# One core, Trainium2: attention's outputs made transposed, four column tiles for the state space's outputs, and the last team's sum split in two pairs

## The chip, the cores and the metric

One core of one Trainium2 chip. The metric is the device time of one execution in microseconds (us), smaller is better. Engines: TensorE (PE; its weight loads are shown as PEld), VectorE (DVE), ScalarE (ACT), GpSimd (POOL), and the queue that SyncE issues transfers on (SPq). All data are float32, for which every matrix product of the program is two instructions on TensorE, and a transpose one.

## The reference

One layer over 320 tokens: 256 of a prompt and 64 of a sample. Every token goes through three branches, gated and summed, then through a mixture of experts.

```python
h = rmsnorm(x, g_attn); proj = h @ w_in          # u, q_lat, kv_lat, k_pe, q_mem, gate logits
# A: s5_branch(u): diagonal complex state space, 32 groups of 16 channels, 64 states each
#    h_t = ab * h_{t-1} + bu_t;  y = Re(c h) + d u;  out = GLU(gelu(y) @ w_glu)
# B: o = softmax(q k^T / sqrt(96), chunk mask) v, 8 heads of 64;  @ w_o_mla
# C: o = softmax(q_mem mem_k^T / sqrt(128)) mem_v, 4 heads of 128;  @ w_o_mem
x = x + (gA * br_a + gB * br_b + gC * br_c) @ w_out
# experts: 4 groups of 8; a token's best group, its two best experts there
x = x + sum_e gate_e * ((silu(h2 @ w_e1[e]) * (h2 @ w_e3[e])) @ w_e2[e])     # 32 experts, 1024 -> 256 -> 1024
```

## The kernel before

Tokens stand in three tiles (`TILES`): two of 128 for the prompt and a short one of 64 for the sample (`t` = 0, 1, 2). Weights come through three slots `W0` to `W2`; later seven slots `E13` hold experts' up-weights (2 MB an expert, in two transfers) and six slots `E2` down-weights (1 MB).

**The middle.** `middle()` (from L188) writes out one list of steps, `MIDDLE`, and each engine runs the same list in this order and does its part of each step. `put` appends a step and adds its `WORK` to `spent`; when `spent` reaches `due`, `start_turn` puts a turn of the state space in. So a step more or less in the list moves the turns against the other steps. Results in PSUM rotate over five banks (`RING`), and a bank is written again when its former content was copied out (`emptied`, by the engine that `emptier` names).

**Attention.** The heads of a tile are cut into units, 5 for `mem` (branch C) and 10 for `mla` (branch B). A unit m has the steps S (scores), PT (transposes of the probabilities P) and O (output), in the order S(n), PT(n-1), O(n-2), with fills between them (`gateC`, `gateB`, `gateA`: 16 instructions of 320 columns each). After S VectorE takes the maximum (`scores_max`), ScalarE the exponentials P with their sums; PT waits for these. O is made with tokens on the rows: weights PT, moving the values (L966). VectorE divides by the sums when it copies O out (L1749, L1753). When a tile's O is whole, a step OT transposes it (four instructions, L926) and ScalarE copies it to `oTmem` or `oTmla`.

**The state space.** There are 16 turns. `turn_in(q)`: TensorE makes the inputs of turn q (`s5_turn`, L894 and L895, 32 rows deep each, in different row tiles and banks), VectorE rotates them by four products and two sums (L1681 to L1688); `turn_scan` (L1698) twice; `turn_back` (L1706 to L1715) writes a state in `hS[q % 4]`. In each odd turn from 3 on, `s5_y` (L883) multiplies two finished states by `wC`, each onto 32 of 128 rows of bank `YB`, so four turns fill it; `y_skip` on VectorE takes it up. `last_y` does the last two states.

**The end of the middle.** `LAST_WOUT` is the last product with `w_out`. The loads of the experts 4 to 6 wait for it on SyncE (`done(LAST_WOUT[NT - 1])`), since their slots lie where the weights were. Routing follows.

**The experts.** Pairs p = 0 to 15, two pairs a team of 128 rows. For each pair TensorE does `up(p)` (64 instructions of 256 columns onto 32 rows each, four column tiles), `hid_transpose`, `down(p)` (16 of 512 columns, L1217), between these the former team's sums into X (`add_team`, `sum_products`, L1227; VectorE adds them to X, L2080) and the next team's rows. `load_up(e)` waits until `up` has used the slot, `load_down(e)` likewise. The last expert's weights come in halves with semaphores of their own. After `down(15)` the last team's sums are made in five steps (`SUMS`): weights `WG` 128 deep, which is both pairs' rows of `yb` at once; VectorE adds all of them to X and SyncE stores X in five transfers (L621).

```python
for n in range(len(units) + 2):                       # attention_order
    if n < len(units): yield "S", n
    if 1 <= n <= len(units): yield "PT", n - 1
    if n >= 2:
        yield "O", n - 2
        if n - 1 == len(units) or units[n - 1][1] != units[n - 2][1]:
            yield "OT", units[n - 2][1]
```

## Time and profile before

| what | value |
|---|---|
| median of 3 runs | 646.52 us (645.71 to 647.54) |
| profiled execution | 645.93 us, its span 644.1 us |
| TensorE busy | 611.7 us, 95% of the span |
| VectorE, ScalarE, GpSimd busy | 329.3, 170.9, 149.7 us |
| chain that ended last | TensorE 83%, transfers' queue 9%, VectorE 4% |
| moved by DMA | 150.55 MB, 147.12 MB of it read |
| granted TensorE clock | 0.999 of full speed |

The span is that of the profiled execution; busy time is what the engine spent in instructions, so a busy TensorE may still be one that fills few of its rows. The chain follows the last instruction back to what released each step. A row of a timeline gives the start in us, the time in us, engine, line, operation, written and read tiles, rows and columns, how many instructions were merged, and in brackets the idle time before it with what ended it.

### The profile page before, as it was taken

The page shows a single profiled execution, that of the slowest core. Times are in us where ns is not written, and L with a number is a line of the kernel's source. Part 1 is how long each engine was busy: PE and PEld are TensorE (multiplying, and loading weights), DVE is VectorE, ACT ScalarE, POOL GpSimd, SP SyncE. Part 2 cuts the span into 40 slices and gives each one's busy share as a digit, 9 for nine tenths or more (in the row PEclk, how much of TensorE's full clock was granted, in tenths as well). Part 3 has the DMA queues.
Part 4 walks back from the last instruction along what each step waited for, and adds up shares of the span by engine and source line. Part 5 has one row for each costly group of instructions (what it writes and reads, how often), then busy time and mean ns, then how long its engine had stood idle before and what let it go on. Part 6 is the DMA issues. An engine that isn't in the chain of part 4 may idle for free.

```text
span 644.1 us, 9883 instructions
## 1 busy us (share of the span) xinstructions
PE 611.7 (95%) x3674; PEld 378.5 (59%) x3674; DVE 329.3 (51%) x878; ACT 170.9 (27%) x540; POOL 149.7 (23%) x341
## 2 busy tenths in 40 slices
PE   9999999999999999999999999998999999986785
PEld 6788867776556667666677767853443343332341
DVE  2434846868874588783133322675435335334233
ACT  5534234321678433221100101121221121120100
POOL 1695726733584433410000000000000000000000
PEclk9999999999999999999999999999999999999999
DMA  9783553222301523323389991098999999999993
GB/s 301 176 284 115 193 159 99 66 67 93 101 2 33 168 95 99 99 66 98 107 236 404 399 386 64 10 383 345 417 417 413 418 416 417 417 418 417 416 409 126
DMA packets 61681, 150.55 MB, mean 234 GB/s; under 512 B 12352, under 2 KB 40448, under 8 KB 53696
## 3 DMA queue, kind: packets, MB, share of 16 engines
q1 hardware_dynamic: 61632, 149.89, 62.7%
q8 instruction: 31, 0.51, 0.3%
q14 instruction: 18, 0.15, 0.1%
HBM read 147.12 MB, written 2.76 MB: 233 GB/s over the span
## 4 chain that ended last, share of the span: by engine, by line
PE 83%; SPq 9%; DVE 4%; DMA 2%; ACT 1%; issue 1%
PE PS L819 30%; PE PS L829 20%; SPq L704 6%; PE PS L1188 5%; PE PS L1096 5%; PE PS L1227 3%; SPq L708 3%; PE PS L1217 3%; DMA E<-in_w_e 2%; PE PS L943 2%; PE PS L966 2%; PE PS L894 2%; PE PS L883 1%; PE PS L800 1%; PE PS L1008 1%; PE PS L951 1%
## 5 line engine op out<-in xcount | busy, mean ns | idle before, releaser
L819 PE MATMUL PS<-hT,W 128*128 128x320 f32 x448 | 125.9, 436 | 0.0
L819 PEld LDWEIGHTS PS<-hT,W 128*128 128x128 f32 x448 | 83.6, 190 | 37.5 <-issue 5.2
L1188 PE MATMUL PS<-E,xT 128*32 128x256 f32 x1024 | 58.6, 379 | 9.5 <-issue 8.4
L1188 PEld LDWEIGHTS PS<-E,xT 128*32 128x32 f32 x1024 | 35.4, 110 | 36.9 <-issue 20.4
L2152 POOL TENSOR_SCALAR means<-sums 128x4 f32<-128x4 f32 (+3 forms) x35 | 7.9, 225 | 189.2 <-ACT junk L1325 188.2
L1096 PE MATMUL PS<-h,S 128*128 128x512 f32 (+1 forms) x96 | 48.2, 625 | 0.7 <-DVE S L1939 0.7
L1227 PE MATMUL PS<-yb,WG 128*128 128x512 f32 (+1 forms) x96 | 40.9, 622 | 4.0 <-DVE X L2080 3.1
L829 PE MATMUL PS<-W,hT 128*128 128x256 f32 (+5 forms) x256 | 41.7, 353 | 0.0
L2080 DVE TENSOR_TENSOR X<-X,PS 128x512 f32<-128x512 f32 (+1 forms) x48 | 32.9, 686 | 8.3 <-PE PS L1227 6.7
L829 PEld LDWEIGHTS PS<-W,hT 128*128 128x128 f32 (+1 forms) x256 | 31.5, 163 | 8.4 <-issue 1.3
L829 PE MATMUL PS<-W,mergedT 128*128 128x384 f32 (+3 forms) x192 | 35.7, 381 | 0.0
L819 PE MATMUL PS<-uT,W 128*128 128x320 f32 x128 | 34.6, 432 | 0.0
L1217 PE MATMUL PS<-E,hidT 128*32 128x512 f32 x256 | 31.0, 598 | 2.6 <-issue 2.0
L2062 DVE COPY yb<-PS 64x512 f32<-64x512 f32 x16 | 10.9, 684 | 41.2 <-PE PS L1217 41.2
L1096 PEld LDWEIGHTS PS<-h,S 128*128 128x128 f32 (+1 forms) x96 | 15.5, 187 | 27.9 <-issue 26.7
L2153 POOL TENSOR_TENSOR rstd<-means,halves 128x4 f32<-128x4 f32 (+3 forms) x35 | 31.0, 885 | 2.9
L819 PEld LDWEIGHTS PS<-uT,W 128*128 128x128 f32 x128 | 24.3, 190 | 10.1
L829 PEld LDWEIGHTS PS<-W,mergedT 128*128 128x128 f32 (+1 forms) x192 | 24.2, 163 | 9.8 <-issue 0.3
L829 PE MATMUL PS<-W,memT 128*128 128x256 f32 x128 | 28.3, 381 | 0.0
L1227 PEld LDWEIGHTS PS<-yb,WG 128*128 128x128 f32 (+1 forms) x96 | 11.4, 170 | 28.0 <-DVE X L2080 15.4
L1421 ACT ACTIVATE P<-PS,soft 128x256 f32<-128x256 f32 (+2 forms) x30 | 13.3, 450 | 49.6 <-DVE soft L1744 21.8
L829 PEld LDWEIGHTS PS<-W,memT 128*128 128x128 f32 x128 | 24.1, 190 | 4.0 <-issue 0.9
(313 smaller groups left out, 959.0 us busy)
## 6 DMA issues: line engine op xcount, KB each, us to landing
E<-in_w_e SPq DMA_DIRECT2D x93, 1024.0 KB, 21.8
W<-in_w_in SPq DMA_DIRECT2D x7, 1536.0 KB, 7.2
W<-in_w_in SPq DMA_DIRECT2D x7, 1024.0 KB, 6.6
W<-in_w_mem_kv SPq DMA_DIRECT2D x4, 1024.0 KB, 6.1
W<-in_w_glu SPq DMA_DIRECT2D x4, 768.0 KB, 8.0
W<-in_w_out SPq DMA_DIRECT2D x2, 1536.0 KB, 15.4
E<-in_w_e SPq DMA_DIRECT2D x6, 512.0 KB, 18.8
X<-in_x_prompt SPq DMA_DIRECT2D x4, 512.0 KB, 4.4
```

Source lines behind the costliest of these rows:

```text
L704: sp.dma_start(E13[e % UPS][:, n, k0:k1, :], e13_src[n][:, e, k0:k1, :]) .then_inc(up_loaded[e % UPS] if k0 == 0 else s["last_up_loaded"], 16)
L708: sp.dma_start(E2[e % DOWNS][:, j0:j1, :], e2_src[:, e, j0:j1, :]) .then_inc(down_loaded[e % DOWNS] if j0 == 0 else s["last_down_loaded"], 16)
L819: ins = mm(out[:, 0:TOK], w[:, k, cols:cols + 128], rhs[:, k, :], start=(k == 0), stop=(k == kt - 1))
L829: ins = mm(out[r:r + n, 0:part.stop - part.start], lhs[:, k, f:f + n], w[:, k, c0 + part.start:c0 + part.stop], start=(k == 0), stop=(k == ...
L894: mm(PS[:, BU, 0:TOK], wB[r:r + 32, 0, t, :], uT[r:r + 32, t, :], start=True, stop=True)
L1096: return mm(PS[:, banks + c, :], S[0:n, t, :], h2[0:n, t, 512 * c:512 * c + 512], start=(t == 0), stop=(t == NT - 1))
L1188: ins = mm(PS[r:r + B, 2 + par, 0:FF], xT[:, k, place_ + B * n:place_ + B * n + B], E13[slot][:, :, k, 128 * j:128 * j + 128], start=(k == ...
L1217: ins = mm(PS[r:r + B, 5, :], hidT[:, par, 64 * n + B * j:64 * n + B * j + B], E2[slot][:, j, 512 * c:512 * c + 512], start=(j == 0), stop ...
L1227: ins = mm(PS[r:r + rows_, sum_bank(n), :], WG[:, f:f + rows_], yb[:, c, :], start=True, stop=True)
L1421: ins = fn(P[0:n, m % 2, nk * h:nk * h + nk], src[0:n, nk * h:nk * h + nk], ACT.Exp, bias=soft[0:n, w, 0, h:h + 1], scale=scale, accum_out ...
L2080: yield V_.tensor_tensor(x, x, PS[r:r + rows_, sum_bank(n), :], ALU.add)
L2153: g_.tensor_tensor(rstd[0:rows_, n, 0:heads], means[0:rows_, n, 0:heads], halves[0:rows_, 0:heads], ALU.pow)\
```

## The change

- **Attention.** The steps OT go. O is now made transposed: the values are the weights and PT moves, so the result has features on the rows: 128 of them a head in `mem`, in `mla` two heads side by side in column tiles of 64. ScalarE copies it straight to `oTmem` or `oTmla`. The division by the sums moves before the transposes: VectorE multiplies P in place (`shares(m)`), in its part of step S of unit m+1, for the last unit in its own PT. PT waits for `shares_ready`.
- **State space.** `s5_y(t)` takes four states at once onto four column tiles, in turns 5, 9, 13 and in `last_y`; `hS` has five buffers (`STATES`).
- **Last team.** Before `up(15)`, TensorE puts columns 0 to 511 of X (times the identity) and the share of pair 14 of four of the six results in PSUM (`rows_so_far`, `add_last_but_one`); the other two come around `hid_transpose(15)`. `down(15)` works in halves of 256 columns into banks 5 and 4, which VectorE and ScalarE copy 128 rows high. `add_last` adds pair 15, 64 deep, alternating row tiles; ScalarE copies columns 0 to 511 to X, VectorE adds columns 512 to 1023, and SyncE stores six parts.
- **Loads.** Up-weights of expert 30 are loaded after the down-weights of 28 and 29; those of expert 31 as 6/8 and 2/8.

```diff
+STATES = 5
...
-            if n - 1 == len(units) or units[n - 1][1] != units[n - 2][1]:
-                yield "OT", units[n - 2][1]
...
-            if step == "OT":
-                whole.append(m)
-                continue
...
-                for k0, k1 in ((0, KD),) if e < NE - 1 else ((0, KD // 2), (KD // 2, KD)):
+                for k0, k1 in ((0, KD),) if e < NE - 1 else ((0, LAST_K), (LAST_K, KD)):
...
-                if 2 * p + UPS < NE:
+                ups, downs = (range(2 * p + n, min(2 * p + 2 + n, NE)) for n in (UPS, DOWNS))
+                if ups:
                     sp.wait_ge(s["ab_full"], p + 1)
-                    for e in range(2 * p, min(2 * p + 2, NE - UPS)):
-                        load_up(e + UPS)
-                if 2 * p + DOWNS < NE:
+                for e in ups:
+                    if e != NE - 2:
+                        load_up(e)
+                if downs:
                     sp.wait_ge(s["y_mm"], p + 1)
-                    for e in range(2 * p, min(2 * p + 2, NE - DOWNS)):
-                        load_down(e + DOWNS)
+                for e in downs:
+                    load_down(e)
+                if NE - 2 in ups:
+                    load_up(NE - 2)
...
-            for n, (t, cs) in enumerate(SUMS):
+            for i, t in enumerate(LAST_TILES):
                 f, rows_ = TILES[t]
-                sp.wait_ge(s["sum_added"], added_by(len(SUMS) * (TEAMS - 1) + n))
                 dst = o["y_p"][f:f + rows_, :] if t < 2 else o["y_s"]
-                c0, c1 = 512 * cs[0], 512 * cs[-1] + 512
-                store(dst[:, c0:c1], X[0:rows_, t, c0:c1])
+                for c, by in enumerate(("last_act", "last_dve")):
+                    sp.wait_ge(s[by], i + 1)
+                    store(dst[:, 512 * c:512 * c + 512], X[0:rows_, t, 512 * c:512 * c + 512])
             st.after(stored[-1])
...
-            def s5_y(q):
-
-                t = q // 4
-                pe.wait_ge(s["h_state"], q + 2)
-                if q % 4 == 0 and t > 0:
+            def s5_y(t):
+
+                pe.wait_ge(s["h_state"], 4 * t + 4)
+                if t > 0:
                     pe.wait_ge(s["y_skipped"], t)
                 for c in range(2):
-                    for n in (q, q + 1):
-                        r = 32 * (n % 4)
-                        ins = mm(PS[r:r + 32, YB, 0:TOK], wC[:, c, t, r:r + 32], hS[:, n % 4, c, :], start=(c == 0), stop=(c == 1))
+                    for n in range(4):
+                        r = 32 * n
+                        ins = mm(PS[r:r + 32, YB, 0:TOK], wC[:, c, t, r:r + 32], hS[:, (4 * t + n) % STATES, c, :], start=(c == 0), stop=(c == 1))
...
-                if q % 2 == 1 and q > 1:
-                    s5_y(q - 3)
+                if q % 4 == 1 and q > 1:
+                    s5_y(q // 4 - 1)
...
-                        emptied((kind, "S", m))
+                        pe.wait_ge(s["shares_ready"], unit0 + m + 1)
...
-                        dv = MD if mem_ else VH
-                        for x in range(nh):
+                        across_ = 1 if mem_ else 2
+                        for i in range(heads // across_):
                             for b, rows_ in enumerate(kb):
-                                for c in range(parts):
-                                    h = h0 + nh * c + x
+                                for r in range(across_):
+                                    c, x = divmod(across_ * i + r, nh)
+                                    h = h0 + across_ * i + r
                                     at = 128 * (x * len(kb) + b) + n * c
                                     if mem_:
-                                        rhs = mv[0:rows_, t // 2, b, MD * h:MD * h + MD]
+                                        values = mv[0:rows_, t // 2, b, MD * h:MD * h + MD]
                                     else:
-                                        rhs = V[0:rows_, (0 if t < 2 else 2) + b, VH * h:VH * h + VH]
-                                    ins = mm(out[n * c:n * c + n, dv * x:dv * x + dv], PT[0:rows_, m % 2, at:at + n], rhs,
+                                        values = V[0:rows_, (0 if t < 2 else 2) + b, VH * h:VH * h + VH]
+                                    w = 128 // across_
+                                    ins = mm(out[w * r:w * r + w, n * i:n * i + n], values, PT[0:rows_, m % 2, at:at + n],
...
+            def last_down(slots, par):
 
                 for j in range(2):
-                    if j == 1 and second is not None:
-                        pe.wait_ge(*second)
+                    if j == 1:
+                        pe.wait_ge(s["last_down_loaded"], 16)
+                    for half, bank_ in enumerate((5, 4)):
+                        for c in range(2):
+                            for n, slot in enumerate(slots):
+                                r, at = 64 * c + B * n, 512 * c + 256 * half
+                                ins = mm(PS[r:r + B, bank_, 0:256], hidT[:, par, 64 * n + B * j:64 * n + B * j + B],
+                                         E2[slot][:, j, at:at + 256], start=(j == 0), stop=(j == 1))
...
+            def last_place(t, c):
+                bank_, r = LAST_BANKS[t, c]
+                return PS[r:r + TILES[t][1], bank_, :]
+
+            def rows_so_far():
+
+                pe.wait_ge(s["sum_added"], ADDS * (TEAMS - 1))
+                pe.wait_ge(s["weights_ready"], TEAMS)
+                pe.wait_ge(s["weights_moved"], 1)
+                for t in LAST_TILES:
+                    n = TILES[t][1]
+                    mm(last_place(t, 0), ident[0:n, 0:n], X[0:n, t, 0:512], start=True, stop=False)
+
+            def add_last_but_one(t, c):
+                f, n = TILES[t]
+                mm(last_place(t, c), WG[0:64, f:f + n], yb[0:64, c, :], start=(c == 1), stop=False)
+
+            def add_last():
+                pe.wait_ge(s["last_y"], 2)
+                for t in LAST_TILES:
+                    f, n = TILES[t]
+                    for c, weights in enumerate((last_weights[:, f:f + n], WG[64:128, f:f + n])):
+                        mm(last_place(t, c), weights, last_rows[64 * c:64 * c + 64, :], start=False, stop=True).then_inc(s["last_full"], 1)
...
+                    rows_so_far()
+                    pe.wait_ge(s["y_dve"], PAIRS - 1)
+                    pe.wait_ge(s["y_act"], PAIRS - 1)
+                    for t in LAST_TILES[0:2]:
+                        for c in range(2):
+                            add_last_but_one(t, c)
                 up(p)
+                if p == PAIRS - 1:
+                    add_last_but_one(LAST_TILES[2], 0)
...
+                    add_last_but_one(LAST_TILES[2], 1)
                 down(p)
-            add_team(TEAMS - 1, range(len(SUMS)))
+            add_last()
...
+                def shares(m):
+                    _, nh = across(units[m])
+                    nk = sum(key_blocks(units[m]))
+                    w = soft[:, (unit0 + m) % 4]
+                    dve.wait_ge(*emptied_at(UNIT_NO[kind, "S", m]))
+                    link(V_.reciprocal(w[:, 2, 0:nh], w[:, 1, 0:nh]))
+                    p = P[:, m % 2, 0:nh * nk].rearrange("p (h k) -> p h k", h=nh)
+                    V_.tensor_tensor(p, p, w[:, 2, 0:nh, None].broadcast_to([128, nh, nk]), ALU.mult).then_inc(s["shares_ready"], 1)
+
+                if step == "PT" and m == len(units) - 1:
+                    shares(m)
                 if step == "S":
+                    if m > 0:
+                        shares(m - 1)
...
-                    link(V_.reciprocal(w[:, 2, 0:nh], w[:, 1, 0:nh]))
-                    n = TILES[t][1]
-                    for c in range(parts):
-                        h, r = h0 + nh * c, slice(n * c, n * c + n)
-                        st.mark(V_.tensor_tensor(O[0:n, t, dv * h:dv * (h + nh)].rearrange("p (h d) -> p h d", h=nh), src[r],
-                                                 w[r, 2, 0:nh, None].broadcast_to([n, nh, dv]), ALU.mult),
-                                s["emptied_dve"] if c == parts - 1 else None)
...
+                    V_.tensor_copy(last_rows[:, 0:256], PS[:, 5, 0:256]).then_inc(s["last_y"], 1)
...
-            add_team(TEAMS - 1, range(len(SUMS)))
+            for i, t in enumerate(LAST_TILES):
+                bank_, r = LAST_BANKS[t, 1]
+                n = TILES[t][1]
+                dve.wait_ge(s["last_full"], 2 * i + 2)
+                V_.tensor_tensor(X[0:n, t, 512:D], X[0:n, t, 512:D], PS[r:r + n, bank_, :], ALU.add).then_inc(s["last_dve"], 1)
```

**Order of VectorE, the last unit of `mem`.** Before, around turn 6 (L1681 to L1688 are `turn_in`, L1743 and L1744 the maximum of the last S, L1749 and L1753 the division of an O, L1698 `turn_scan`):

```order
L1743 TENSOR_REDUCE soft<-PS 128x2 [waits psum_full]
L1744 TENSOR_SCALAR soft<-soft 128x2 [waits dve_step]
L1749 RECIPROCAL soft<-soft 128x2 [waits psum_full]
L1753 TENSOR_TENSOR O<-PS,soft 128x256 [waits dve_step]
L1681 TENSOR_TENSOR rotA<-PS,tab_133 128x320 [waits bu_full,turn_tables]
L1682 TENSOR_TENSOR rotB<-PS,tab_133 128x320
L1683 TENSOR_TENSOR rotA<-PS,tab_133 128x320
L1684 TENSOR_TENSOR rotB<-PS,tab_133 128x320
L1686 TENSOR_TENSOR rotA<-rotA,rotB 128x320 [waits dve_step]
L1688 TENSOR_TENSOR rotA<-rotA,rotB 128x320 [waits dve_step,bu_free]
L1698 SCALAR_TENSOR_TENSOR rotB<-s5tmp,rotA 128x256 [waits dve_step]
L1698 SCALAR_TENSOR_TENSOR rotB<-s5tmp,s5par,rotA 128x64
```

The scans follow the turn directly. Now the same place (L1728 to L1735 and L1801, L1802; L1781 and L1783 are `shares`, first of unit 3, then of unit 4):

```order
L1781 RECIPROCAL soft<-soft 128x2 [waits emptied_act]
L1783 TENSOR_TENSOR P<-P,soft 128x512 [waits dve_step]
L1801 TENSOR_REDUCE soft<-PS 128x2 [waits psum_full]
L1802 TENSOR_SCALAR soft<-soft 128x2 [waits dve_step]
L1728 TENSOR_TENSOR rotA<-PS,tab_132 128x320 [waits bu_full,turn_tables]
L1729 TENSOR_TENSOR rotB<-PS,tab_132 128x320
L1730 TENSOR_TENSOR rotA<-PS,tab_132 128x320
L1731 TENSOR_TENSOR rotB<-PS,tab_132 128x320
L1733 TENSOR_TENSOR rotA<-rotA,rotB 128x320 [waits dve_step]
L1735 TENSOR_TENSOR rotA<-rotA,rotB 128x320 [waits dve_step,bu_free]
L1781 RECIPROCAL soft<-soft 128x2 [waits emptied_act]
L1783 TENSOR_TENSOR P<-P,soft 128x512 [waits dve_step]
```

The divisions of O are gone from behind the maximum and the scans. Shares 3 stands before the maximum, and shares 4, for which the last PT waits, stands directly behind the whole of `turn_in 6`.

**Order of TensorE at the same place.** L819 and L814 are gates, L894/L895 and L888/L889 the turn, L926 an OT, L951 and L939 the transposes of P, L966 and L956 the O. Before, from OT of tile 0:

```order
L926 MATMUL PS<-cst,O 128x128 [waits emptied_dve,emptied_act]
L926 MATMUL PS<-cst,O 128x128 x3
L951 MATMUL PS<-cst,P 128x128 [waits emptied_act]
L951 MATMUL PS<-cst,P 128x128 x3
L966 MATMUL PS<-mv,PT 128x128 [waits emptied_act,emptied_dve]
L966 MATMUL PS<-mv,PT 128x128 x3
L894 MATMUL PS<-uT,wB 128x320 [waits bu_free]
L895 MATMUL PS<-crossed_146,wB 128x320
L819 MATMUL PS<-hT,W_145 128x320 [waits emptied_act,chunk_loaded2]
L819 MATMUL PS<-hT,W_145 128x320 x7
L951 MATMUL PS<-cst,P 128x128 [waits emptied_act]
L951 MATMUL PS<-cst,P 128x128 x3
```

A gate stands between the turn and PT 4. Now, from the transposes of unit 3:

```order
L939 MATMUL PS<-cst,P 128x128 [waits shares_ready,emptied_act]
L939 MATMUL PS<-cst,P 128x128 x3
L956 MATMUL PS<-PT,mv 128x128 [waits emptied_act]
L956 MATMUL PS<-PT,mv 128x128 x3
L814 MATMUL PS<-hT,W_144 128x320 [waits emptied_act,chunk_loaded2]
L814 MATMUL PS<-hT,W_144 128x320 x7
L888 MATMUL PS<-uT,wB 128x320 [waits bu_free]
L889 MATMUL PS<-crossed_145,wB 128x320
L939 MATMUL PS<-cst,P 128x128 [waits shares_ready,emptied_act]
L939 MATMUL PS<-cst,P 128x128 x3
L956 MATMUL PS<-PT,mv 128x128 [waits emptied_act]
L956 MATMUL PS<-PT,mv 128x128 x3
```

The gate (gateC 3) has moved ahead of the turn, and PT 4 follows the turn at once.

**Order of TensorE at the end.** Now, from the last two y products of pair 14 to the first product of `up(15)` (L1255 `rows_so_far`, L1259 `add_last_but_one`, L1178 `up`):

```order
L1218 MATMUL PS<-E_4_157,hidT 32x512
L1218 MATMUL PS<-E_5_158,hidT 32x512
L1272 TENSOR_LOAD ovi [waits ov_ready]
L1272 ISA x2
L1255 MATMUL PS<-X,cst 64x512 [waits weights_moved,weights_ready,sum_added]
L1255 MATMUL PS<-X,cst 128x512 x2
L1259 MATMUL PS<-yb,WG 64x512 [waits y_act,y_dve]
L1259 MATMUL PS<-yb,WG 64x512
L1259 MATMUL PS<-yb,WG 128x512 x2
L1178 MATMUL PS<-E_2_153,xT 32x256 [waits xt_ready,hid_ready,up_loaded3,up_loaded2]
```

Before, `up(15)` followed the y products of pair 14 directly; seven products of 512 columns stand between them now.

## Rows read from the trace of the kernel before

**Rows 1.** table of stretches (us: engines' busy us, clock, DMA share, GB/s)

```profile
35.00:421.00 386.00, 384.88 (x1927) 268.99 (x1925) 218.93 (x567) 115.66 (x421) 133.72 (x294) 1.00 0.43 144
390.00:417.00 27.00, 27.00 (x196) 20.73 (x194) 11.67 (x45) 4.47 (x8) 1.51 (x4) 1.00 0.00 1
...
440.00:600.00 160.00, 147.20 (x1261) 63.35 (x1254) 67.95 (x176) 27.59 (x56) 0.00 (x0) 1.00 1.02 417
```

**Rows 2.** chain that ended last, from 616 us (start us, us, what)

```profile
616.86 15.23 DMA E<-in_w_e
...
634.11 4.72 PE PS L1227 x12
...
638.86 0.69 DVE X L2080
```

**Rows 3.** timeline of TensorE, turn 13

```profile
262.29 0.53 PE L894 MATMUL PS<-uT,wB 32*128 32x320 f32 x1
...
263.03 1.27 PE L883 MATMUL PS<-hS,wC 128*32 128x320 f32 x8
264.23 0.66 PE L951 MATMUL PS<-cst,P 128*128 128x128 f32 x4
```

**Rows 4.** timeline of TensorE, second half of `up(15)`

```profile
627.19 1.93 PE L1188 MATMUL PS<-E,xT 128*32 128x256 f32 x32 [0.68 <-DMA E<-in_w_e]
```

**Rows 5.** timeline of TensorE, OT 0, PT 3, O 2 and S 5 of `mla`

```profile
255.26 0.60 PE L926 MATMUL PS<-cst,O 128*128 128x128 f32 x4
255.69 0.60 PE L951 MATMUL PS<-cst,P 128*128 128x128 f32 x4
256.13 1.00 PE L966 MATMUL PS<-V,PT 128*128 128x64 f32 x8
256.97 1.08 PE L943 MATMUL PS<-kT,qT 96*128 96x256 f32 x4
```

**Rows 6.** timeline of TensorE, O of the last unit of `mem`

```profile
147.71 1.09 PE L966 MATMUL PS<-mv,PT 128*64 128x128 f32 x16
148.73 0.53 PE L894 MATMUL PS<-uT,wB 32*128 32x320 f32 x1
```

**Rows 7.** timeline of VectorE, `mla`, before the maximum of unit 4

```profile
252.60 0.15 DVE L1749 RECIPROCAL soft<-soft 128x4 f32<-128x4 f32 x1
252.79 0.42 DVE L1753 TENSOR_TENSOR O<-PS,soft 128x256 f32<-128x256 f32 x1
...
253.97 0.68 DVE L1740 SCALAR_TENSOR_TENSOR PS<-PS,early 128x512 f32<-128x512 f32 x1
```

**Rows 8.** groups of VectorE by form (busy us, mean ns, idle before)

```profile
L1792 DVE TENSOR_TENSOR KQ<-KQ,rstd 128x384 f32<-128x384 f32 x4 | 2.2, 556 | 2.9 <-POOL rstd L2153 2.8
```

**Rows 9.** timeline of TensorE: turn 4, PT 0 and PT 1 of `mem`

```profile
109.90 0.53 PE L894 MATMUL PS<-uT,wB 32*128 32x320 f32 x1
...
113.81 0.66 PE L951 MATMUL PS<-cst,P 128*128 128x128 f32 x4
...
119.48 0.60 PE L951 MATMUL PS<-cst,P 128*128 128x128 f32 x4
```

**Rows 10.** timeline of VectorE: `turn_in 4`, maximum of S 1, of S 2

```profile
110.83 0.49 DVE L1681 TENSOR_TENSOR rotA<-PS,tab 128x320 f32<-128x320 f32 x1 [3.80 <-PE PS L895]
...
113.42 0.68 DVE L1743 TENSOR_REDUCE soft<-PS 128x2 f32<-128x512 f32 x1
...
120.06 0.68 DVE L1743 TENSOR_REDUCE soft<-PS 128x2 f32<-128x512 f32 x1
```

**Rows 11.** timeline of TensorE, pair 14's transposes and y products, pair 15's

```profile
621.05 0.62 PE L1160 MATMUL PS<-cst,Sg 128*128 128x128 f32 x3
622.03 1.92 PE L1217 MATMUL PS<-E,hidT 128*32 128x512 f32 x16 [0.36 <-issue]
...
631.02 2.18 PE L1217 MATMUL PS<-E,hidT 128*32 128x512 f32 x16 [0.54 <-DMA E<-in_w_e]
```

**Rows 12.** stores from X on SyncE's queue (ns; first and last start)

```profile
L621 SPq DMA_DIRECT2D out_y_p<-X x4: 417/493/576, 637.4 to 639.6; - x4
```

More of the change, by code:

```diff
@@ L263, in middle @@
             fill()
-    whole = attention("mem", MEM_UNITS, 1)
+    attention("mem", MEM_UNITS, 1)
     for t in range(NT):
@@ L271, in middle @@
         put("qlT", t)
-    for t in whole:
-        put("mem", "OT", t)
     for j in range(len(KEYS)):
@@ L288, in middle @@
     held, pace, due = False, LATE_PACE, spent
-    whole = attention("mla", MLA_UNITS, 1)
+    attention("mla", MLA_UNITS, 1)
     fill(1)
-    for t in whole:
-        put("mla", "OT", t)
     while turn < GP:
@@ L343, in emptier @@
     if unit[0] in ("mem", "mla"):
[L344 removed]
+        return "act"
     return "dve" if unit[0].startswith("out") else "act"
@@ L719, in _ @@
             sp.dma_start(brow[:, NG:], a["b_re"][0].rearrange("g e -> (g e)").partition_broadcast(128)).then_inc(s["router_loaded"], 16)
-            done(("mla", "OT", NT - 1))
+            done(("mla", "O", len(MLA_UNITS) - 1))
             load_up(0)
@@ L921, in attention @@
                     out = begin((kind, step, m))
-                    if step == "OT":
-                        n = TILES[m][1]
-                        emptied((kind, "O", max(k for k, x in enumerate(units) if x[1] == m)))
-                        for j in range(4):
-                            ins = nc.tensor.transpose(out[:, n * j:n * j + n], O[0:n, m, 128 * j:128 * j + 128], ident[0:n, 0:n])
-                        end(ins)
-                        return
-                    _, t, h0, nh = units[m]
+                    unit0 = 0 if mem_ else len(MEM_UNITS)
+                    _, t, h0, heads = units[m]
                     f, n = TILES[t]
@@ L1019, in branch @@
                     if d == 0:
-                        emptied(("mem" if kind == "outC" else "mla", "OT", NT - 1))
+                        emptied(("mem", "O", len(MEM_UNITS) - 1) if kind == "outC" else ("mla", "O", len(MLA_UNITS) - 1))
                     feature_major((kind, d), use(f"{kind}{g}"), col, oTmem if kind == "outC" else oTmla, 4)
@@ L1042, in _ @@
                 elif kind == "last_y":
-                    s5_y(GP - 2)
+                    s5_y(GP // 4 - 1)
             pe.wait_ge(s["z_ready"], 4)
@@ L1406, in attention @@
                 unit0, oT = (0, oTmem) if kind == "mem" else (len(MEM_UNITS), oTmla)
-                if step == "OT":
-                    f, n = TILES[m]
-                    empty(oT[:, :, f:f + n], full((kind, "OT", m))[:, 0:4 * n].rearrange("p (j n) -> p j n", j=4))
+                t, n = units[m][1], 128
+                if step == "O":
+                    f, n = TILES[t]
+                    j0, nj = (x * (MD if kind == "mem" else VH) // 128 for x in units[m][2:])
+                    empty(oT[:, j0:j0 + nj, f:f + n], full((kind, "O", m))[:, 0:nj * n].rearrange("p (j n) -> p j n", j=nj))
                     return
-                t, n = units[m][1], 128
                 _, nh = across(units[m])
@@ L1726, in attention @@
             def attention(kind, units, step, m):
[L1727 to L1728 removed]
                 unit0 = 0 if kind == "mem" else len(MEM_UNITS)
[L1730 to L1735 removed]
+                def shares(m):
[8 more added lines that the diff above has]
+                    shares(m)
+                if step == "S":
+                    if m > 0:
+                        shares(m - 1)
+                    t, n = units[m][1], 128
+                    _, nh = across(units[m])
+                    nk = sum(key_blocks(units[m]))
+                    w = soft[:, (unit0 + m) % 4]
                     src = full((kind, "S", m))[:, 0:nh * nk]
```

75 lines of the change are left out of this document (40 added, 35 removed).

## The prediction

> **What bounds the kernel now.** I read the table of stretches first, then the chain that ended last, then the timelines at the places that the diff touches. From 35 to 421 us TensorE is busy 384.9 of 386.0 us [rows 1]: a microsecond less of its work there, or a microsecond of waiting more, is a microsecond of time. From 390 to 417 us the DMA engines move nothing, because the loads of experts 4 to 6 wait for `done(LAST_WOUT...)`; from 440 us on they are busy without a gap at 417 GB/s [rows 1]. So the middle sets when the last stream of expert weights begins, the stream sets when it ends, and a shift of the middle goes through to the end whole. The chain ends with the last landing at 616.86 + 15.23 = 632.09 us, the last team's products from 634.11 (4.71 us) and a VectorE addition from 638.86 to 639.55 [rows 2]. What follows is stores. The profiled execution took 645.93 us (span 644.1); the median is 646.52, 0.6 above. The sum is made against 645.93 and then moved by 0.6.
>
> **The change, part by part: TensorE work that goes.**
> State-space output: a call of `s5_y` now is 8 instructions, two column tiles wide, and lasts 264.23 - 263.03 = 1.20 us [rows 3]. There are eight calls (64 instructions). The new call has 16 instructions, four column tiles wide. That four run side by side is seen in the experts: 32 instructions of 256 columns onto 32 rows take 1.93 us [rows 4], 0.06 each, so 16 of 320 columns take 16 x 0.06 x 320/256 = 1.2 us. Four calls fewer: **-4.8** (ends -4.4 and -5.0).
> Transposes of O ("OT"): four of them take 255.69 - 255.26 = 0.43 us [rows 5], six groups: **-2.6**.
> O of the prompt tiles in `mla`: 8 instructions now take 256.97 - 256.13 = 0.84 us, 0.105 each although only 64 columns stream [rows 5]; with operands swapped they have 64-row outputs and 128 columns, two side by side, as the 16 at 147.71 have: (148.73 - 147.71)/16 = 0.064 [rows 6]. 8 x 0.064 = 0.51, six units: **-2.0**. The last `mem` unit goes the other way: its 16 now fill all 128 output rows with 64 columns, at 0.105 instead of 0.064: **+0.7**.
> Together -8.7 us of TensorE work.
>
> **What it adds: a VectorE step before the transposes of P.** Until now a PT (the transposes of the probabilities P) waited for ScalarE's exponentials alone; now it waits for `shares_ready`. `shares(m)` is a reciprocal, 0.2 us until the next can start (252.60 to 252.79) [rows 7], and a multiplication of 128x512: 128x384 takes 0.56 and 128x256 0.42 [rows 7, 8], so 0.70 here. Ready 0.9 us after VectorE gets to it; VectorE itself is held 0.8. VectorE runs in order, and the turns' work stands ahead of it:
> - PT 0 of `mem`. Turn 4 on TensorE starts at 109.90 and on VectorE at 110.83; VectorE is through at 113.42, where share 0 now begins; ready 114.35. TensorE is there at 113.81 [rows 9, 10]: wait 0.55.
> - PT 1. Share 1 stands behind the whole of turn 4, which ended at 120.06 [rows 10]. With share 0 ahead: 120.06 + 0.8 + 0.9 = 121.8; TensorE is there at 119.48 + 0.55 = 120.0 [rows 9]: wait 1.8.
> - PT 4 of `mem`, the last unit. By the order, `turn_in 6` now stands directly before it, on TensorE and on VectorE (it stood before gateC 3). VectorE begins a turn 0.93 us after TensorE does and needs 113.42 - 110.83 = 2.6 for it [rows 9, 10], then the share 0.9: ready 4.4 us after the turn's start. TensorE needs 0.74 for the turn [rows 3]: wait **3.7**. Nothing covers it.
> - PT 3 of `mla`. VectorE begins the mask of unit 4 at 253.97 without idling before it [rows 7]. Shares 1 and 2 are added before it (+1.6), the normalisations of O 0 and O 1 go (2 x (0.2 + 0.35) = -1.1), and share 3 comes: ready at 255.4. TensorE, which gets to PT 3 at 255.69 now [rows 5], arrives earlier by one `s5_y` call (1.2), one OT (0.43) and two O (0.66): 253.4. Wait 2.0. The second gate behind it needs a PSUM bank whose exponentials are late by as much: 0.5 more.
> Elsewhere in both attentions a PT has a gate (4.4 us) between itself and the S that releases the share, and VectorE has caught up.
> Together **+8.5**. Ends: 3.7 alone, if VectorE keeps up elsewhere (its work beside GpSimd's between 115 and 119 us is stretched, and may stretch less), and 11, if the multiplications are stretched as those were. I take the sum by rows. ScalarE takes over the eviction of O: 15 copies instead of 6, against waits of microseconds there; nothing. The fifth state buffer lets `turn_back` run as before; nothing. The middle nets **-0.2**.
>
> **The end.** Loads: up-weights of expert 30 now come behind down-weights 28 and 29, and expert 31's come as 6/8 and 2/8. The bytes are the same, the last landing stays; the y products of pair 14 no longer wait. In its place TensorE gets work. After the transposes at 621.05 (0.62) [rows 11] come the y products of pair 14, 1.9 us [rows 11], to 623.6. Then, ahead of `up(15)`: three products of the identity with X, and four of pair 14's rows, of which the two of the short tile run side by side. That is six slots of 2 x 512 columns; the 12 instructions from 634.11 are ten such half slots in 4.71 us with 0.2 of latency [rows 2], so 0.43 to 0.45 a half slot, 0.86 a slot: 5.2 us. `up(15)` starts at 628.8, not in two halves at the landings; its 64 instructions take 3.7, to 632.4. Now it ends at 627.19 + 1.93 = 629.12 [rows 4]. From there to the y products is 631.02 - 629.12 = 1.9 [rows 11]: 634.3; two more products of pair 14 lie beside ScalarE's and VectorE's work in it. These are 32 of 256 columns, 1.9 [rows 4]: 636.2. The copies are halved, 0.42 instead of 0.69: 636.6, and 0.15 to TensorE: 636.8. Last products: six slots of 64 rows deep, two side by side in row tiles. The turn shows such pairs: 2 pairs of 320 columns take 263.03 - 262.29 = 0.74 [rows 3], 0.37 a pair, 0.10 above the streaming alone (0.27). So 6 x (0.43 + 0.10) + 0.2 = 3.4 (ends 2.8 with no loss, 5.2 with no overlap): 640.2. VectorE adds until 640.9, against 639.55 [rows 2]. Stores: the last was issued at 639.6 and one takes 0.5 [rows 12]; ScalarE's and VectorE's halves of the last tile are now ready together and the second is issued about 641.4. So the end is **+1.8** (ends +1.2 and +3.6), not the gain of about 1.1 that the shorter last products would give if `up(15)` still started at its landing.
> The Trainium skill, TensorEngine Tiling (Array Packing), section Restrictions and Gotchas, says that different row tiles have to write to different PSUM banks. The short tile's two last products are in different row tiles and share bank 6. By that rule they would not overlap, and the sum would be 0.4 us higher; the turn's pairs write to two banks, so no row here tests it.
>
> **Sum.** -8.7 + 8.5 + 1.8 = +1.6: 645.93 + 1.6 = 647.5 for the profiled execution, **648.1** beside the median.
>
> **The rivals.**
> 1. Slower: the waits on the shares grow. Between 115 and 120 us VectorE's scans and products took longer than elsewhere; if the 512-wide multiplications of five `mem` units are stretched by half, the waits grow by 1 to 1.5, and with the last products overlapping poorly (+1.5) it is 650.6. It decides from 0.4 us above the sum. For it: VectorE is what every PT waits for now. Against: most shares have a gate's cover.
> 2. Only the wait behind turn 6 is left, since VectorE has caught up at the other three: -8.7 + 3.7 + 1.8 = -3.2, 643.3. Against it: VectorE had no idle time before 120.06 and 253.97.
> 3. The end gains after all, because `up(15)` starts near its landing: -0.2 - 1.1, 645.2. It needs the seven inserted products to take 2 us instead of 5.2.
> 4. The change does all that it says and no wait shows: -8.7 - 1.1, 636.7. Turn 6 speaks against it by order, not by speed.
> 5. It doesn't do what it says: the four column tiles run two wide. Each of four calls lasts 2.4: no gain of 4.8, 652.9. The experts' 32-row products speak against it.
>
> **How the numbers follow.** About 0.3% (1.9 us) is what a measurement of this kernel can tell from no change. The sum as worked has 0.60, with 646.7 to 650 as its own spread; its middle lies 0.3 us under the bound to slower, so 0.38 of it is within and 0.22 above. Rival 1 has 0.15, rival 2 0.10, rivals 3 and 4 0.06 each, rival 5 0.03. Faster: 0.16; within: 0.44; slower: 0.40. The range from 643.2 (rival 2) to 650.6 (rival 1) leaves out rivals 4 and 5 and half of rival 1's worse side.
>
> **What would show it.** `s5_y` as four groups of 16 at 1.2 us; no transposes of O; the waits of TensorE on VectorE's P in 90 to 292 us together about 8, the longest 3.7 right behind turn 6; the stream of expert 4 beginning at 417, within half a microsecond; `up(15)` about 3 us after its weights; the last products in 3.4 us. Wrong would be: that wait under 2 us, or `up(15)` beginning before 627, or last products over 4.5.

## The result and the profile after

The changed kernel takes 650.62 us (median of 5 runs, 649.45 to 650.69), 4.1 us more than the 646.52 before; the ratio is 1.0058, 95% interval 1.0046 to 1.0070. It is **slower by 0.6%**. Its profiled execution took 650.69 us (span 648.8), 4.8 more than the one before. TensorE is busy longer than the 611.7 us before, although it has some 8 us less to do in the middle and some 6 us more in the last team, and the mean granted clock fell from 0.999 to 0.988. From the page (busy time by engine, and the chain that ended last, where before TensorE had 83% and the transfers' queue 9%):

```profile
PE 615.8 (95%) x3684; PEld 377.4 (58%) x3684; DVE 328.1 (51%) x870; ACT 174.3 (27%) x553; POOL 151.4 (23%) x341
...
PE 86%; DVE 9%; issue 2%; ACT 2%; DMA 1%; POOL 0%; SPq 0%; DVEq 0%; ACTq 0%
```

The stretches of the changed kernel (columns as in [rows 1], so TensorE's clock is the third from the right) show where:

```profile
140.00:145.00 5.00, 3.05 (x13) 1.63 (x11) 1.83 (x5) 0.44 (x1) 0.00 (x0) 1.00 0.20 81
145.00:150.00 5.00, 3.40 (x14) 3.24 (x15) 4.86 (x13) 0.98 (x2) 0.00 (x0) 0.50 0.00 0
150.00:155.00 5.00, 5.00 (x18) 3.35 (x17) 1.41 (x4) 0.00 (x0) 3.82 (x11) 0.82 0.00 0
```

TensorE idles 3.5 us, and from 145.0 us, still in that wait, to 151.7 its granted clock is 0.50, which is 1.2 GHz. No such stretch lies in the middle of the kernel before. This is about half of what the mean clock lost; the rest is two stretches among the experts, from 442 to 446 and from 585 to 589 us. Behind the second TensorE still idles 1.76 us before `up(13)` and again before `up(14)`, so these two do not reach the end. TensorE's waits by line (us in total, times, longest), and its timeline at this place:

```profile
PE PS L939 <- DVE P L1783: 6.9, 4, 3.5
PE PS L814 <- ACT P L1458: 0.2, 1, 0.2
```

```profile
142.62 0.43 PE L888 MATMUL PS<-uT,wB 32*128 32x320 f32 x1
...
146.60 1.09 PE L939 MATMUL PS<-cst,P 128*128 128x128 f32 x4 [3.54 <-DVE P L1783]
147.48 1.92 PE L956 MATMUL PS<-PT,mv 128*128 128x128 f32 x8
149.19 5.79 PE L814 MATMUL PS<-hT,W 128*128 128x320 f32 x16
154.81 1.89 PE L956 MATMUL PS<-PT,mv 128*128 128x64 f32 x16
156.63 0.53 PE L888 MATMUL PS<-uT,wB 32*128 32x320 f32 x1
```

The wait in brackets is the one behind turn 6. VectorE at the same place goes through the turn and then makes the last unit's shares, without idling between them:

```profile
143.17 0.49 DVE L1728 TENSOR_TENSOR rotA<-PS,tab 128x320 f32<-128x320 f32 x1 [9.19 <-PE PS L889]
...
145.57 0.15 DVE L1781 RECIPROCAL soft<-soft 128x2 f32<-128x2 f32 x1
145.76 0.69 DVE L1783 TENSOR_TENSOR P<-P,soft 128x512 f32<-128x512 f32 x1
```

The transposes behind it take 1.09 us, against 0.60 to 0.66 for such a group before [rows 9]; with the O, the gate and the last O it is 10.0 us from 146.60 to 156.63. At half clock from 146.6 to 151.7, TensorE did in 5.1 us what takes half of that at full clock: 2.5 us lost. The stream of experts 4 to 6 on SyncE's queue starts at 419.56 here:

```profile
419.56 21.01 SPq L695 DMA_DIRECT2D E<-in_w_e  x10
```

Before, it started at 417.09:

```profile
417.09 20.99 SPq L704 DMA_DIRECT2D E<-in_w_e  x10
```

So **2.5 of the 4.8 us are lost by the end of the middle**, and 2.3 in the last team: VectorE's last sum ends at 644.37 instead of 639.55 [rows 2], 4.8 later. The chain of waits at the end, from the y products of pair 14, is TensorE's work and VectorE's copy and sum, with no landing in it:

```profile
624.51 1.85 PE PS L1218 x16
626.36 2.91 PE PS L1255 x6
629.28 2.92 PE PS L1259 x8
632.19 3.59 PE PS L1178 x64
635.78 1.05 PE PS L1259 x2
636.84 0.32 PE PS L1187
637.15 1.05 PE PS L1259 x2
638.21 1.91 PE PS L1208 x32
640.12 0.02 issue
640.14 0.43 DVE xg L2111
640.57 0.04 issue
640.62 3.04 PE PS L1266 x12
643.66 0.02 issue
643.68 0.69 DVE X L2156
```

The last landing, which was the first link before [rows 2], is no part of it. `up(15)` starts 5.83 us behind the end of the y products of pair 14 (632.19 - 626.36).

### The profile page after: what moved, and what is told of

Read it like the earlier page. It is cut to its first block, busy times and chain, and to the rows that moved or that the text cites. A ratio compares the mean times of both kernels' runs of the same rounds, so it can differ in the third digit from the quotient of the medians.

```text
span 648.8 us, 9903 instructions
## 1 busy us (share of the span) xinstructions
PE 615.8 (95%) x3684; PEld 377.4 (58%) x3684; DVE 328.1 (51%) x870; ACT 174.3 (27%) x553; POOL 151.4 (23%) x341
## 4 chain that ended last, share of the span: by engine, by line
PE 86%; DVE 9%; issue 2%; ACT 2%; DMA 1%; POOL 0%; SPq 0%; DVEq 0%; ACTq 0%
PE PS L814 27%; PE PS L824 20%; PE PS L1178 8%; PE PS L1086 7%; PE PS L1218 5%; PE PS L1228 4%; PE PS L888 2%; PE PS L956 2%; DVE X L2131 1%; PE PS L1139 1%; PE PS L931 1%; PE PS L998 1%; DVE rotB L1745 1%; PE PS L939 1%; PE PS L1259 1%
## 5 line engine op out<-in xcount | busy, mean ns | idle before, releaser
L814 PE MATMUL PS<-hT,W 128*128 128x320 f32 x448 | 127.2, 439 | 0.2 <-ACT P L1458 0.2
L814 PEld LDWEIGHTS PS<-hT,W 128*128 128x128 f32 x448 | 84.4, 192 | 38.1 <-issue 6.2
L1178 PE MATMUL PS<-E,xT 128*32 128x256 f32 x1024 | 60.0, 387 | 6.9 <-issue 6.6
L1178 PEld LDWEIGHTS PS<-E,xT 128*32 128x32 f32 x1024 | 35.8, 112 | 35.8 <-issue 19.0
L1228 PE MATMUL PS<-yb,WG 128*128 128x512 f32 (+1 forms) x84 | 36.2, 625 | 3.1 <-DVE X L2131 3.1
L814 PE MATMUL PS<-uT,W 128*128 128x320 f32 x128 | 34.6, 432 | 0.0
L2131 DVE TENSOR_TENSOR X<-X,PS 128x512 f32<-128x512 f32 (+1 forms) x42 | 28.8, 686 | 6.8 <-PE PS L1228 5.3
L814 PEld LDWEIGHTS PS<-uT,W 128*128 128x128 f32 x128 | 24.3, 190 | 10.1
L2282 POOL TENSOR_TENSOR turnt<-tab 128x64 f32<-128x64 f32 (+2 forms) x48 | 25.4, 530 | 3.8
```

Source lines behind the costliest of these rows:

```text
L814: ins = mm(out[:, 0:TOK], w[:, k, cols:cols + 128], rhs[:, k, :], start=(k == 0), stop=(k == kt - 1))
L1178: ins = mm(PS[r:r + B, 2 + par, 0:FF], xT[:, k, place_ + B * n:place_ + B * n + B], E13[slot][:, :, k, 128 * j:128 * j + 128], start=(k == ...
L1228: ins = mm(PS[r:r + rows_, sum_bank(n), :], WG[:, f:f + rows_], yb[:, c, :], start=True, stop=True)
L2131: yield V_.tensor_tensor(x, x, PS[r:r + rows_, sum_bank(n), :], ALU.add)
L2282: st.mark(tt(t1, T[:, :, 0:n], cn, ALU.mult))
```

## The experiments

The medians stand against 647.0 to 647.1 us for the kernel before, measured beside them (645.1 to 647.8). Its runs lie in two groups, up to 646.7 and from 647.1 on, so a difference of medians is good to about half a microsecond only. Four runs took the change apart, four took the waits and the tail apart, four followed up.

The profiles give a sharper figure for the middle: the time from the start of turn 0 on TensorE to the start of the stream of experts 4 to 6. It leaves out what differs before turn 0, and it is 361.21 us in all four profiles that have the middle of before.

| kernel | turn 0 | stream | between | against before |
|---|---|---|---|---|
| before | 55.88 | 417.09 | 361.21 | |
| `tail_only`, `tail_no_identity`, `order_of_loads` | 56.67, 56.87, 57.06 | 417.88, 418.08, 418.27 | 361.21 | 0 |
| changed | 56.35 | 419.56 | 363.21 | +2.0 |
| `mid_only` | 56.49 | 419.94 | 363.45 | +2.2 |
| `s5_only` | 56.55 | 413.02 | 356.47 | -4.7 |
| `att_only` | 56.02 | 421.97 | 365.95 | +4.7 |
| `turn_later` | 56.39 | 413.55 | 357.16 | -4.1 |
| `shares_sooner` | 56.48 | 413.34 | 356.86 | -4.4 |
| `mid_shares_sooner` | 56.25 | 411.54 | 355.29 | -5.9 |
| `shorter_wait` | 56.86 | 415.92 | 359.06 | -2.2 |
| `pace_12_5` | 56.45 | 409.18 | 352.73 | -8.5 |
| `pace_11_5` | 56.56 | 413.06 | 356.50 | -4.7 |

**The two halves of the program.** `mid_only` is the changed kernel with the last team of before; `tail_only` the reverse.

```diff
-            add_last()
+            add_team(TEAMS - 1, range(len(SUMS)))
```

(for `mid_only`, with its loads, copies and stores.)

> The change's attention and state-space parts, with the last team, its loads and its sums as in the kernel before. Theory: the middle loses by itself. In the changed kernel's trace the stream of experts 4 to 6 begins at 419.56 us against 417.09, 2.5 later, of which 0.5 had gone before 35 us, where both run the same instructions. So 2.0 to 2.5 above before: 648.5 to 649.1, the wait behind turn 6 about 3.5 us, and the granted clock at half speed for some 6 us right behind it. Rival: only the tail costs, the late stream being made up in its waits for landings: 646.5, with a stream that begins late all the same.

Measured: 648.99 (647.65 to 649.80), ratio 1.0033 [1.0021, 1.0044], **+2.0**. The stream starts at 419.94, the wait is 3.55, the clock is at half from 145.6 to 152.0 us. The rival falls: the late stream is not made up, the last landing is at 635.27 against 632.09.

> The kernel before with only the change's last team: its loads, the seven products ahead of up(15), the halved copies, the split sum. Theory: the inserted products delay up(15) by their own length whether or not the middle is late. The changed kernel's last VectorE addition ends at 644.37 against 639.55, 4.8 later, less the 2.5 of the stream: +2.3, so 648.8 (648.4 to 649.2), with up(15) starting about 5.8 us behind the end of pair 14's y products. Rival: the tail is a gain (shorter last products, 3.0 instead of 4.7) and only looks late because the middle was: 645.2 to 646.5.

Measured: 650.10 (649.51 to 650.38), ratio 1.0051 [1.0037, 1.0065], **+3.1**, more than the theory's 2.3. `up(15)` starts 5.83 us behind the y products as expected, and VectorE's last sum ends at 642.32; with the stream 0.8 late (417.88), that is 2.0 above before. The rest is behind it: in this profile one of the four stores of the prompt took 1.77 us to issue, in the changed kernel none over 0.59.

```profile
L624 SPq DMA_DIRECT2D out_y_p<-X x4: 446/516/1772, 641.6 to 643.2; - x4
```

(ns, smallest, median, largest.) Whether every run of `tail_only` has that isn't known (all six lie within 0.9 us); it would explain why the two halves sum to 5.0 and the whole is 4.1.

**The two parts of the middle.** `s5_only` is the kernel before with the new `s5_y(t)` and this in place of the eight calls (the fourth is in `last_y`):

```diff
+STATES = 4
...
-                if q % 2 == 1 and q > 1:
-                    s5_y(q - 3)
+                if q % 4 == 0 and q > 0:
+                    s5_y(q // 4 - 1)
```

> The kernel before with s5_y on four column tiles, four calls instead of eight; with O still in memory a fifth state buffer does not fit, so there are four buffers and the call stands in turns 4, 8 and 12 (three states old at least by a whole turn) and in last_y. Theory: TensorE is full in the middle and each call that goes is 1.2 us: -4.8, 641.7 (641.2 to 642.3), the stream beginning at 412.3. Rival: the freed time turns into waits on VectorE, which runs the turns, or on the ring: 643.5 or more.

Measured: 642.11 (640.85 to 643.04), ratio 0.9929 [0.9913, 0.9945], **-4.9**, and the middle is 4.7 shorter in the profile. The theory's -4.8 holds.

`att_only` has the attention hunks and `s5_y(q)` as before, four state buffers.

> The kernel before with only the attention part: O made transposed, no OT, the shares multiplied into P before the transposes; s5_y as before (eight calls, four buffers). Theory: the attention part alone costs what the two others hide. Work -3.2 (six OT -2.6, the O of mla -1.5, the last O of mem +0.8), waits on the shares +7 and half clock behind the longest +2.5: 652 to 653.5. Rival: without the state-space saving TensorE comes later to each transpose and VectorE has caught up, so only the wait behind turn 6 is left and the clock keeps: 646.5 to 648.

Measured: 651.91 (650.86 to 653.05), ratio 1.0085 [1.0068, 1.0101], **+4.9**. Its waits on the shares are 5.6 us in three (the one before PT 3 of `mla` doesn't show), the longest again 3.55, with half clock for less long, 148.4 to 151.8. So the change is a gain of 4.9 and two losses, attention and last team. They don't simply add up: -4.9 and +4.9 would leave the middle at nothing, and `mid_only` is at +2.0. The traces have the difference: `mid_only` waits 1.3 us longer on the shares, and the half clock costs it 2.6 us (146.74 to 152.0, halved) where it costs `att_only` 1.7. Why is not tested; without the state space's saving TensorE comes later to these places.

**The wait behind turn 6.** `turn_later` moves one turn by one step:

```diff
+        nonlocal held
...
             if m == len(units) - 1 and step in ("PT", "O"):
+                held = step == "PT"
                 fill(1)
+                held = False
```

> The changed kernel, but turn 6 may not be put in between the last gate and the last unit's transposes in mem; it comes right behind the transposes (the same flag moves a turn at the last unit of mla, where none stands there). Theory: the 3.5 us wait goes, and with it the stretch at half clock behind it (1.6 to 2.5 us): 650.6 - 5.1 to 6.1 = 644.5 to 645.5, with the clock at 1.00 from 100 to 160 us. Rival 1: the clock falls for the mix of work, not for the wait: only 3.5 come back, 647.1. Rival 2: the turn does the same damage one place on: 649 or more.

Measured: 644.55 (644.38 to 645.54), ratio 0.9970 [0.9959, 0.9981]: **6.1 us under the changed kernel** for a wait of 3.5. The waits on the shares are 3.4 in three, the clock is 1.00 from 100 to 300 us. The middle is 6.05 us shorter than the changed kernel's. Both rivals fall. The half clock hangs on the wait, and it costs about 2.5.

**All waits.** `shares_sooner` changes VectorE's order, nothing on TensorE:

```diff
-                if step == "PT" and m == len(units) - 1:
-                    shares(m)
+                if step == "PT" and m < len(units) - 1:
+                    shares(m + 1)
                 if step == "S":
-                    if m > 0:
-                        shares(m - 1)
...
+                    if m == 0:
+                        shares(0)
```

> The changed kernel with the shares of unit m+1 made in VectorE's part of PT(m), ahead of the gates and turns that follow, and those of unit 0 in its own S. The list of steps is the changed kernel's. Theory: all four waits on the shares (0.6, 1.5, 3.5, 1.4) and the second gate's 0.2 go, with the stretch at half clock: 7.5 + 2.5 less, 640.6 (640 to 642). Rival: VectorE now stands waiting for ScalarE's exponentials, the turns behind it come later, and TensorE waits for bu_free or the next maximum instead: 643.5 or more.

> The same shares, with the last team of the kernel before. Theory: TensorE's work in the middle is 8.1 us less than before and nothing waits: stream of experts 4 to 6 from about 409, last landing at 624, 638.9 (638 to 640), and 2 to 3 below shares_sooner. Rival: the last team's new form pays once the middle is short: this one is at or above shares_sooner.

Measured: `shares_sooner` 642.69 (641.91 to 644.26), ratio 0.9938 [0.9925, 0.9952]; `mid_shares_sooner` 641.27 (640.63 to 642.91), ratio 0.9922 [0.9909, 0.9936]. Both are over 2 above their theories and outside their ranges; for `shares_sooner` that is most of the way to its rival, and `mid_shares_sooner`'s rival falls. At turn 6, with TensorE's instructions in the changed kernel's order and no wait, the clock is 1.00. The waits on the shares are 0.2, but a new one of 1.8 stands at the gate behind S 5 of `mla`. That gate needs the bank with the scores of unit 4, and VectorE now has turn 12, the shares of unit 3 and the scans ahead of that unit's maximum:

```profile
255.75 6.10 PE L814 MATMUL PS<-hT,W 128*128 128x320 f32 x16 [1.82 <-ACT P L1458]
```

The two have the same middle, and the same wait was followed by this stretch in the profile of `shares_sooner`:

```profile
255.00:260.00 5.00, 4.25 (x10) 2.95 (x11) 4.12 (x10) 2.27 (x10) 2.73 (x8) 0.66 0.00 0
```

and by this one in that of `mid_shares_sooner`:

```profile
255.00:260.00 5.00, 4.49 (x18) 2.98 (x18) 3.88 (x10) 2.27 (x9) 2.97 (x9) 1.00 0.00 0
```

The last team of before is the better one here too, by 1.4 where 2 to 3 were expected. In the two profiles, 3.4 us apart, 1.6 of the difference is this stretch.

**A shorter wait.** `shorter_wait` is the changed kernel with one line in VectorE's `turn_in`, behind the second product (and the shares of that unit gone from their place):

```diff
+                if q == 6:
+                    attention("mem", MEM_UNITS, "shares", len(MEM_UNITS) - 1)
```

> The changed kernel with the shares of mem's last unit in the middle of turn 6 on VectorE, behind two of its six instructions, so that the wait behind the turn is 1.6 us shorter, about 1.9 instead of 3.5. Theory: a wait has its own length as price, and the granted clock may or may not fall behind it: 649.0 if it falls as now, 646.5 if it never does, and between them with a wide spread if it falls in some runs. Rival: the clock falls only behind waits as long as 3.5: 646.5 in all runs, spread below 1 us.

Measured: 648.09 (646.29 to 650.73 in 12 runs), ratio 1.0027 [1.0013, 1.0041]. The profiled run, 646.79, has a wait of 1.95 and the clock at 1.00 behind it:

```profile
145.51 0.63 PE L939 MATMUL PS<-cst,P 128*128 128x128 f32 x4 [1.95 <-DVE P L1785]
145.97 1.06 PE L956 MATMUL PS<-PT,mv 128*128 128x128 f32 x8
146.87 4.47 PE L814 MATMUL PS<-hT,W 128*128 128x320 f32 x16
151.17 1.89 PE L956 MATMUL PS<-PT,mv 128*128 128x64 f32 x16
153.00 0.53 PE L888 MATMUL PS<-uT,wB 32*128 32x320 f32 x1
```

The same work takes 153.00 - 145.51 = 7.5 us here and 10.0 in the changed kernel, which is the 2.5. The runs without a profile show only their mean clock, and that goes with the time: three runs with 0.992 or 0.993 took 646.3 to 646.8, seven with 0.990 or 0.991 took 647.9 to 648.8, two with 0.989 took over 650. That speaks for the theory (the clock falls in some runs), though it doesn't show the place, and the last two lie above the 649.0 that one fall would give. The spread of 4.4 us alone says less: `order_of_loads`, which has no wait on shares, spreads over 3.4 in 12 runs.

**The last team.** `tail_no_identity` is `tail_only` without the products of `rows_so_far`; VectorE adds both halves.

> The kernel before with the change's last team, but without the three products of the identity with X: VectorE adds both halves of each tile to X instead (six additions). TensorE has 2.9 us less ahead of up(15). Theory: the inserted products are what delays the end; up(15) starts 2.9 sooner, the sums end 2.9 sooner, VectorE's six additions of 0.69 take 1.1 us longer than the three do: 650.1 - 1.9 = 648.2 (647.7 to 648.8). Rival: up(15) waits for its weights anyway, so the removed products bring nothing and the additions cost: 651.

Measured: 648.47 (646.86 to 650.66), ratio 1.0024 [1.0011, 1.0037], in the stated range, but not by the stated steps. The products of pair 14 now waited 1.0 for VectorE's copy of pair 14's rows, `up(15)` started at 628.88 instead of 630.13, and it ran at a lower clock:

```profile
625.44 3.45 PE L1273 MATMUL PS<-yb,WG 64*64 64x512 f32 x8 [1.00 <-DVE yb L2120]
628.81 4.83 PE L1195 MATMUL PS<-E,xT 128*32 128x256 f32 x64
```

VectorE's last sum ended at 643.55, not sooner but 1.2 later than in `tail_only`. So it doesn't settle what the three products cost. `order_of_loads` leaves everything but the loads as before:

> The kernel before with the change's order of loads alone (up-weights of expert 30 behind the down-weights of 28 and 29, those of expert 31 as 6/8 and 2/8). The bytes and the last landing are the same, and TensorE waits for the last landing. Theory: no difference, 646.5 to 647.5, with pair 14's y products no longer waiting 0.4 us. Rival: the up-weights of expert 30 land later and up(15) with them: 648.5 or more, which would be part of tail_only's 3.1.

Measured: 647.26 (645.88 to 649.31), ratio 1.0009 [0.9997, 1.0022]. The loads alone do nothing that these runs can tell.

**The version that follows.** `pace_12_5` and `pace_11_5` are `mid_shares_sooner` with one number changed:

```diff
-PACE, LATE_PACE = 13.5, 11.0
+PACE, LATE_PACE = 13.5, 12.5
```

> mid_shares_sooner with the turns of the second attention set 12.5 apart instead of 11, which puts each of turns 11 to 15 right behind an S or a gate and turn 12 behind the S of unit 4: VectorE then makes that maximum before the turn's six instructions. Theory: the last wait there (1.8 us, the gate's bank waiting for late exponentials) goes, and with it what the clock sometimes takes behind it: 641.3 - 1.8 to 2.5 = 638.8 to 639.5, stream from about 409.7. Rival: the wait shows again at another unit, since VectorE has the same work in the same time: 641.

> The same with 11.5 between the turns: turn 11 behind an S, turn 12 right behind the transposes of unit 2. Theory: VectorE reaches the maximum of unit 4 as late as now, so the wait stays at 1 to 2 us: 640.5 to 641.3. Rival: it goes here too: 639.

Measured: `pace_12_5` **638.69** (638.31 to 639.60), ratio 0.9879 [0.9863, 0.9895]; `pace_11_5` 641.31 (640.44 to 642.81), ratio 0.9915 [0.9898, 0.9932]. With 12.5 TensorE has no wait on shares or maxima left, the stream starts at 409.18 and the chain of waits ends as before the change, with a landing:

```profile
409.18 2.98 SPq L692 DMA_DIRECT2D E<-in_w_e  x6
```

```profile
609.12 15.27 DMA E<-in_w_e
...
626.42 4.72 PE PS L1210 x12
...
631.16 0.69 DVE X L2065
```

With 11.5 the gate still waits 1.7 us, and in this profile half clock follows it again:

```profile
255.00:260.00 5.00, 4.51 (x11) 3.00 (x12) 4.79 (x12) 1.32 (x5) 2.03 (x6) 0.66 0.00 0
```

Its six runs fall in two groups: three of 640.4 to 640.5 with a mean clock of 0.992 or 0.993, and three of 642.1 to 642.8 with 0.990, of which the profiled one is the fastest. `pace_12_5` is 8.4 us faster than the kernel before and 3.4 faster than `s5_only` (3.7 in the middle); the attention's work alone is 3.3 less (2.6 and 1.5 less, 0.8 more), so it is about the attention's saving without its waits.

## Why the prediction was right and wrong

The direction was right and the size too small. The measured 650.62 is 2.5 above the predicted 648.1, at the upper end of the range (650.6), and it fell to "slower", which had 0.40, not to "within 0.3%", which had 0.44. None of the three signs of being wrong showed, but one of those that should have shown did not: the stream begins at 419.56 and not within half a microsecond of 417.

- **Work that goes, -8.7: right, -8.1.** `s5_y`: 16 instructions four column tiles wide last 1.21 us, `s5_only` gave -4.9 for -4.8 (-4.7 in its middle). OT as said. The O of `mla` gave 1.5 for 2.0: the step O itself fell from 0.84 to 0.59, but the transposes ahead of it rose from 0.44 to 0.53 until the next could start. The last O of `mem` cost 0.8 for 0.7.
- **Waits on the shares, +8.5: nearly right, 7.1.** All four stood where they were put: 0.56 (0.55 expected), 1.48 (1.8), 3.54 (3.7), 1.35 and 0.17 (2.0 and 0.5). A multiplication of 128x512 took 0.69, for 0.70.
- **The step that failed: "wait 3.7. Nothing covers it."** It was priced at its length, and the length was right (3.54). The granted clock was 0.50 from 145.0 to 151.7 us, 2.5 us more, which `turn_later` gave back together with the wait. With these 2.5 the sum would have been 650.6. The Trainium skill, TensorE: Matmul & The Clock Gate, section HAM oscillation — how this bites in real kernels, tells of this: a wait between bursts of products can leave the next burst at half clock. The trace agrees here, and the prediction didn't weigh it. It is no certain price: in `shorter_wait` and `mid_shares_sooner` waits of 1.95 and 1.82 us were not followed by half clock, in `shares_sooner` and `pace_11_5` waits of 1.82 and 1.71 us were.
- **0.5 us had gone before 35 us,** where both kernels run the same instructions; turn 0 begins on TensorE between 55.88 and 57.06 us in the profiles of this case, so this is no effect of the change. Another 0.5 is left over and stays open.
- **The end, +1.8: right in kind, +2.3.** The inserted products took 5.83 for 5.2 (0.49 a half slot, for 0.43 to 0.45), from `up(15)` to the last y products it was 2.4 for 1.9, since the two products of pair 14, 1.05 each, stand one behind the other there and fill more than TensorE had idled at this place (1.03 for VectorE, and 0.54 for a landing [rows 11]); the last products took 3.04 for 3.4. The short tile's two last products, in different row tiles of bank 6, started at the same time (640.62 both), so the 0.4 that the rule on banks in the Trainium skill, TensorEngine Tiling (Array Packing), section Restrictions and Gotchas, would have added did not come. They write to different rows of the bank, 0 to 63 and 64 to 127.

Rival 1 gave 650.6, the measured number, but by stretched multiplications and badly overlapping last products, and neither happened: that it fits is chance. The range reaches up to the measured time only because rival 1 set its upper end, so that is luck too. Rival 2 (only the wait behind turn 6 left) is refuted by the 3.4 us of others in `turn_later`, rival 3 by the inserted products, which took 5.83 us and not 2, rival 4 by the waits, rival 5 by `s5_only`.

## What to carry to other kernels

Where one engine is full, a step that puts another engine's work in front of it can cost that engine's whole backlog at this place, as behind turn 6; look up in the order what stands directly ahead of it, and put the step one place sooner rather than compute it faster. In these runs a wait of TensorE cost its length at least, and 1.5 to 2.6 us more where the clock fell with it; so remove the longest first. And work moved into the gap before a late transfer must fit that gap: here 5.8 us went in ahead of `up(15)`, where TensorE had idled 0.62 us before it and 0.68 in its middle, and TensorE took the transfer's place as the bound.

## What the runs showed of the hardware

The same wait of 1.82 us in the same order of instructions was followed by a granted clock of 0.50 for 3.4 us in one profile (255.5 to 258.9) and by none in another; the gate and what follows until the turn took 6.03 us and 4.48. So whether such a wait costs 1.5 us more differs from one execution to the next, and it can split a kernel's times in two groups, as in `pace_11_5`. All three profiles with a wait of 3.5 us had half clock with it, for 3.4 to 6.7 us. Four column tiles of 32 rows ran the 16 products of `s5_y` in 1.21 us where two tiles ran 8 in 1.20, so the second pair of tiles was free. Behind a gate, the four transposes of a P took 0.43 to 0.44 us until the next step when an O with weights of 128 columns came next, and 0.53 when one with 64 columns or a turn (32 rows deep) did; what in it makes the difference is not shown.
